# A two-layer mixer and expert kernel: the order of the opening, split output products, expert pages in halves

## The chip, the cores and the metric

The kernel runs on one core of a Trainium2 chip, all data in float32 but for a few bf16 masks. A core has five engines with a queue of their own: TensorE (PE in the profile; its weight loads stand apart as PEld), VectorE (DVE), ScalarE (ACT), GpSimd (POOL) and SyncE (SP), which issues most of the loads. Sixteen DMA engines move data between HBM, the large memory, and SBUF, the memory that the engines read. TensorE writes into PSUM. The metric is the device time of one execution in microseconds, the median of several runs.

## The reference

640 tokens (512 latent ones and 128 of a context) of 1024 channels go through two layers. Layer 0 mixes them by a convolution module and a differential attention side by side, layer 1 by a pooling mixer and a short gated convolution. Behind each mixer stands a mixture of 32 experts, two for each token:

```python
h = rmsnorm(x, p['g_norm1'][i]) * (1 + sc1) + sh1
if i % 2 == 0:
    m, k_cur, v_cur = even_mixer(h, p, j, i, rope, kv_in)   # cat([u, o]) @ w_out_e
else:
    m = odd_mixer(h, p, j)                                  # cat([yc, yd]) @ w_out_o
x = x + g1 * m
h = rmsnorm(x, p['g_norm2'][i]) * (1 + sc2) + sh2
y = hmoe(h.reshape(b * t, d), ...)      # top-1 group, top-2 expert
x = x + g2 * y.reshape(b, t, d)
...
hid = jax.nn.silu(xblk @ w_g[e]) * (xblk @ w_u[e])          # one expert, one block of tokens
return hid @ w_d[e]
```

Shifts, scales and gates come from `w_ada` products with a conditioning vector. An expert has three weight matrices of 2 MB (gate, up, down), 201 MB in a layer, and every one is read.

## The kernel before

The program is written engine by engine, each with its own instruction order and explicit semaphores; no scheduler moves anything. Tokens lie in five tiles of 128 (`NT`).

PSUM is used as four pairs of banks, A to D. A table written out by hand (`put`, from line 316) gives every use its pair and its place in that pair's order; `fill` and `take` wait by it. SBUF holds weights in nine slots of 2 MB. Each slot has a counter `slot_full`, raised by 16 for each load. SP's list `dense` names the pages of the dense weights in the order of their loads, and a page is loaded when the last product that read its slot is done (`page_free`).

**Opening.** ScalarE squares the five x tiles; VectorE first copies the turned parameters out of PSUM (line 1403), adds up the first modulation row (`rows_summed`, line 1083), then scales x (`normed`, line 1105). TensorE's opening stands from line 1826: products of `w_ada` pages (`ada_products`, line 1597), turns of the sums (`turned_sums`, line 1606), turns of normalized x, one of eight channel chunks after the other (`first_norm`, line 1620), then the projections (`project`, line 1656), which need the pages `in_e` 0 and 1 and the modulated chunks `hT` that ScalarE and VectorE write.

**Output products.** Behind attention VectorE normalizes the heads, TensorE turns them (`oT`, line 1940), ScalarE copies them out, and the router constant is made (line 1665). `tail` then multiplies tile after tile by the two halves of the output weights (`product`, line 1696: eight channel chunks of 512 columns, the first four from the convolution or pooling side, the last four from heads or the gated convolution). Behind each pair of products VectorE mixes the tile into x and normalizes it, ScalarE copies the turned tile, and TensorE makes its router logits (line 1689). In layer 1 TensorE waits for the last gated channels (`short_conv`) before `tail`.

**Routing.** VectorE makes ranks and tables in many small steps; TensorE adds small products (`ranks_and_table`, lines 1717 to 1732). `keep_busy` (line 1670) runs products into a place that no one reads.

**Experts.** A block is 64 tokens of one expert; four of the 32 positions have a second block, so a layer has 36. A block takes the gate and up products together (`gate_up`, line 1756: eight channel steps, gate and up beside each other), a turn of the hidden values (line 1763), the down products (line 1774). Three experts lie in SBUF. SP loads the next expert into a slot when TensorE is done with it:

```python
def expert(pos, st, done):
    e = sp.value_load(ORD[0:1, bass.ds(pos, 1)], min_val=0, max_val=NE - 1)
    sp.wait_ge(sig("gate_up_done", l), done)
    load(e, st, 0)
    load(e, st, 1)
    sp.wait_ge(sig("down_done", l), done)
    load(e, st, 2)
```

GpSimd gathers the blocks' tokens and scatters the results by indirect DMA.

## Time and profile before

| | us |
|---|---|
| median of three runs | 1820.04 (1819.36 to 1825.13) |
| the profiled execution, its own time | 1817.86 |
| its span, first to last instruction | 1815.6 |
| TensorE busy | 1559.9 (86%) |
| VectorE busy | 616.6 (34%) |
| ScalarE, GpSimd busy | 249.2 (14%), 247.2 (14%) |
| the SP queue's DMA packets, share of 16 engines' span | 67.6% |

The span falls into these stages: opening to 48 us, projections and convolution to some 200, attention to 365, output products and routing to 488, experts of layer 0 to 974, the mixer of layer 1 to 1184, output products and routing to 1296, experts to 1783, the end. The page cuts the span into 40 slices; in both expert stages its DMA row reads 9 (90% or more) in every slice and its rate row 419 to 421 GB/s in nearly all. A busy TensorE says little: matmuls are pipelined, and their time doubles when the granted clock falls from 1.00 (2.4 GHz) to 0.50 (1.2 GHz).

### The profile page before, as it was taken

To read this page: it belongs to the slowest core of one execution; us is meant where nothing else is said; L and a number is where in the kernel's file an instruction comes from. 1 tells how busy PE (TensorE), PEld (TensorE's weight loads), DVE (VectorE), ACT (ScalarE), POOL (GpSimd) and SP (SyncE) were. 2 spreads that over 40 slices of the span, in tenths; PEclk is the share of its full clock that TensorE was granted. 3 is DMA by queue.
4 is the path that set the end of the run, shared out by engine and by line. 5 is a ranking of instruction groups with operands and counts; after the bars stand their busy time and mean duration, and the time that the engine had idled before them with its cause. 6 is when DMAs were issued, how large, how long until landed. Compare 5 with 4: busy or idle time off the path is not lost.

```text
span 1815.6 us, 19429 instructions
## 1 busy us (share of the span) xinstructions
PE 1559.9 (86%) x6780; PEld 727.6 (40%) x6780; DVE 616.6 (34%) x1194; ACT 249.2 (14%) x497; POOL 247.2 (14%) x376
## 2 busy tenths in 40 slices
PE   4999896689898989898984799999898989898982
PEld 2445444545533333333332344545433333333330
DVE  2499546733622112122123220323521212211214
ACT  2111035521100000000002111011000000000001
POOL 0024020000121211211110001000112111121110
PEclk9999999989999999999997899999999999999996
DMA  9753423032599999999995653253699999999984
GB/s 343 270 186 140 156 77 151 24 151 81 190 420 419 419 420 420 420 420 420 421 408 225 216 191 135 93 232 131 258 420 420 419 419 418 419 420 420 419 364 191
DMA packets 115566, 534.12 MB, mean 294 GB/s; under 512 B 15581, under 2 KB 16406, under 8 KB 65066
## 3 DMA queue, kind: packets, MB, share of 16 engines
q1 hardware_dynamic: 92944, 493.45, 67.6%
q0 software_dynamic: 12032, 21.08, 3.1%
q10 hardware_dynamic: 10522, 18.64, 2.9%
q8 instruction: 48, 0.79, 0.2%
q14 instruction: 20, 0.16, 0.0%
HBM read 522.55 MB, written 27.33 MB: 303 GB/s over the span
## 4 chain that ended last, share of the span: by engine, by line
PE 53%; DMA 17%; DVE 4%; issue 3%; ACT 2%; SPq 1%; ACTq 0%; POOLq 0%; DVEq 0%
PE psum_pair_B L1756 22%; DMA scratch<-w_up 15%; PE psum_pair_C L1774 10%; PE psum_pair_C L1696 4%; PE psum_pair_B L1656 4%; PE psum_pair_D L1696 4%; PE psum_pair_A L1656 3%; PE psum_pair_D L1763 1%; DVE scratch L1341 1%; DMA weight_ring<-w_ada 1%; ACT scratch L874 1%; SPq L489 1%; PE psum_pair_C L1597 1%; PE psum_pair_C L1670 1%; PE psum_pair_D L1689 1%
## 5 line engine op out<-in xcount | busy, mean ns | idle before, releaser
L1756 PE MATMUL psum_pair_B<-weight_ring,gates_by_token 128*64 128x512 f32 x1408 | 322.9, 612 | 36.6 <-DMA weight_ring<-w_up 26.0
L1756 PEld LDWEIGHTS psum_pair_B<-weight_ring,gates_by_token 128*64 128x64 f32 x1408 | 119.0, 141 | 234.5 <-issue 234.5
L1341 DVE TENSOR_TENSOR scratch<-psum_pair_B,scratch 128x256 f32<-128x256 f32 x72 | 30.6, 425 | 534.7 <-ACT scratch L874 534.7
L1756 PE MATMUL psum_pair_B<-scratch,gates_by_token 128*64 128x512 f32 x896 | 199.6, 597 | 13.2 <-DMA scratch<-w_up 13.2
L1774 PE MATMUL psum_pair_C<-weight_ring,scratch 128*64 128x512 f32 x704 | 160.8, 597 | 24.9 <-issue 22.5
L682 POOL DMA_INDIRECT expert_rows<-scratch,scatter_rows x72 | 73.4, 1020 | 743.2 <-DVE scratch L1353 743.2
L1656 PE MATMUL psum_pair_A<-scratch,weight_ring 128*128 128x128 f32 (+1 forms) x512 | 143.5, 439 | 4.4 <-DVE scratch L1392 2.8
L874 ACT ACTIVATE scratch<-psum_pair_B 128x256 f32<-128x256 f32 x72 | 27.6, 383 | 866.2 <-PE psum_pair_B L1756 866.2
L1656 PE MATMUL psum_pair_B<-scratch,weight_ring 128*128 128x128 f32 (+1 forms) x512 | 142.2, 436 | 0.0
L1756 PEld LDWEIGHTS psum_pair_B<-scratch,gates_by_token 128*64 128x64 f32 x896 | 76.6, 138 | 132.2 <-issue 132.2
L1435 DVE SCALAR_TENSOR_TENSOR weight_ring<-weight_ring,params 128x655 f32<-128x655 f32 x120 | 117.2, 976 | 5.0 <-DVE gates_by_token L1083 0.9
L1774 PE MATMUL psum_pair_C<-scratch 128*64 128x512 f32 x448 | 102.3, 598 | 15.4 <-issue 11.3
L1353 DVE TENSOR_TENSOR scratch<-psum_pair_C,gates_by_token 128x512 f32<-128x512 f32 x72 | 49.8, 692 | 181.0 <-PE psum_pair_C L1774 181.0
L1656 PEld LDWEIGHTS psum_pair_A<-scratch,weight_ring 128*128 128x128 f32 x512 | 79.2, 192 | 71.2 <-issue 69.4
L1656 PEld LDWEIGHTS psum_pair_B<-scratch,weight_ring 128*128 128x128 f32 x512 | 78.5, 191 | 68.4 <-issue 68.4
L1774 PEld LDWEIGHTS psum_pair_C<-weight_ring,scratch 128*64 128x64 f32 x704 | 55.6, 136 | 99.8 <-issue 99.8
L671 POOL DMA_INDIRECT gates_by_token<-h_rows,gather_rows x68 | 71.1, 1045 | 60.0 <-POOL gather_rows L668 56.4
L1597 PE MATMUL psum_pair_C<-weight_ring,cond_T 128*32 128x512 f32 x368 | 49.5, 661 | 26.0 <-DMA weight_ring<-w_ada 20.4
L1744 PEld LDWEIGHTS psum_pair_A<-square_consts,gates_by_token 128*128 128x128 f32 x288 | 40.4, 209 | 57.7 <-issue 57.7
L1774 PEld LDWEIGHTS psum_pair_C<-scratch 128*64 128x64 f32 x448 | 33.7, 136 | 64.7 <-issue 59.0
L1083 DVE TENSOR_TENSOR gates_by_token<-psum_pair_C,gates_by_token 128x512 f32<-128x512 f32 x23 | 15.8, 686 | 124.1 <-PE psum_pair_C L1597 114.2
L1696 PE MATMUL psum_pair_C<-weight_ring 128*128 128x512 f32 x120 | 55.2, 611 | 0.0
(359 smaller groups left out, 1483.2 us busy)
## 6 DMA issues: line engine op xcount, KB each, us to landing
weight_ring<-w_gate SPq DMA_DIRECT2D x44, 2048.0 KB, 29.4
weight_ring<-w_up SPq DMA_DIRECT2D x44, 2048.0 KB, 33.7
weight_ring<-w_down SPq DMA_DIRECT2D x44, 2048.0 KB, 34.2
weight_ring<-w_ada SPq DMA_DIRECT2D x24, 2048.0 KB, 8.9
scratch<-w_up SPq DMA_DIRECT2D x20, 2048.0 KB, 28.3
scratch<-w_down SPq DMA_DIRECT2D x20, 2048.0 KB, 28.1
scratch<-w_gate SPq DMA_DIRECT2D x20, 2048.0 KB, 22.6
weight_ring<-w_in_e SPq DMA_DIRECT2D x5, 2048.0 KB, 13.2
```

The lines of the kernel that those rows point to most:

```text
L671: pool.indirect_dma_start(XG[par], None, h2_dram, bass.IndirectOffsetOnAxis(GI[par][:, :], 0), bounds_check=2 * TOK - 1, oob_is_err=False) ...
L682: pool.indirect_dma_start(y_dram, bass.IndirectOffsetOnAxis(SI[par][:, :], 0), YR[par], None, bounds_check=4 * TOK - 1, oob_is_err=False). ...
L874: act.activation(SIL[par], bank(B_, par, 256), ACT.Silu).then_inc(sig("silu", l), 1)
L1341: tt(HID[par], PB[B_][:, 512 * par + 256:512 * par + 512], SIL[par], ALU.mult).then_inc(sig("hidden", l), 1)
L1353: tt(YR[par], bank(C_, par), GS[par], ALU.mult).then_inc(sig("y_ready", l), 1)
L1435: stt(UO[:, j, :], UP[:, j, tap:tap + UOW], conv_wT[:, tap, j:j + 1], UO[:, j, :], ALU.mult, ALU.add).then_inc(sig("conv_step", j), 1)
L1597: ins = mm(p[rows, 0:512], condT[:, k, :], w[:, k, :], start=(k < 4), stop=(k >= 4))
L1656: ins = mm(p[:, cols], w[:, k, j * 128:(j + 1) * 128], hT[:, k, cols], start=(k == 0), stop=(k == DC - 1))
L1696: ins = mm(p[:, 0:512], cat(k)[:, t * 128:(t + 1) * 128], w[:, k, :], start=(k == 0), stop=(k == DC - 1))
L1744: ins = pe.transpose(PB[A_][:, 512 * par + c * 128:512 * par + (c + 1) * 128], XG[par][:, c:512:4], ident)
L1756: ins = mm(PB[B_][CAP * q:CAP * (q + 1), 512 * par:512 * par + 512].rearrange("p (u n) -> p u n", u=2), XGT[par][:, at:at + CAP], w[:, :, ...
L1774: ins = mm(PB[C_][CAP * q:CAP * (q + 1), 512 * par:512 * par + 512], HIDT[par][:, at:at + CAP], wd[:, j, 512 * q:512 * (q + 1)], start=(j ...
```

## The change

It has four parts. (1) In the opening VectorE scales x first and then copies the parameters; their three turns go to one PSUM pair with one signal; TensorE turns the chunks of x earlier among the `w_ada` products, and the fourth `w_ada` product moves from pair D to C. (2) `first_half` makes channel chunks 0 to 3 of the first tile's two output products ahead of the rest of them: in layer 0 one ahead of the head turns and one behind them, in layer 1 both ahead of the wait for `short_conv`. The router constant moves to pair A and, in layer 1, ahead of that wait; VectorE takes it after the first tile's mix. (3) Gate and up pages are loaded as two halves of 1 MB each; the first halves wait for the fourth channel step of the block that used the slot, the second ones for the eighth. The counters of those slots rise by 32 for each page. (4) Between ranks and table ten unread products run instead of eight.

```diff
@@ -293,7 +293,7 @@
-            fills = [f + (NE - s // 3 + 2) // 3 for s, f in enumerate(fills)]
+            fills = [f + (1 if s % 3 == 2 else 2) * ((NE - s // 3 + 2) // 3) for s, f in enumerate(fills)]
@@ -483,16 +481,23 @@
-                def load(e, st, kind):
+                def load(e, st, kind, halves=(0, 1)):
+
                     s = 3 * st + kind
-                    src = down_page(e) if kind == 2 else gate_page((wg, wu)[kind], e)
-                    sp.dma_start(gate_slot(s), src).then_inc(slot_full[s], 16)
+                    if kind == 2:
+                        sp.dma_start(gate_slot(s), down_page(e)).then_inc(slot_full[s], 16)
+                    else:
+                        for h in halves:
+                            sp.dma_start(gate_slot(s)[:, h, :], gate_page((wg, wu)[kind], e)[:, h, :]).then_inc(slot_full[s], 16)
...
+                    sp.wait_ge(sig("gate_up_half", l), done)
+                    load(e, st, 0, (0,))
+                    load(e, st, 1, (0,))
                     sp.wait_ge(sig("gate_up_done", l), done)
-                    load(e, st, 0)
-                    load(e, st, 1)
+                    load(e, st, 0, (1,))
+                    load(e, st, 1, (1,))
                     sp.wait_ge(sig("down_done", l), done)
                     load(e, st, 2)
@@ -1398,17 +1403,17 @@
-            for i, (dst, w) in enumerate(((P1, 32), (P2, 125), (P3, 12))):
-                p = take(dve, "par", i + 1)
-                took(dve.tensor_copy(dst[:, :], p[:, 0:w]), "par", i + 1)
-            for i in (1, 2, 3):
-                after(dve, "par", i)
+            normed(0)
+            p = take(dve, "par")
+            for at, dst, w in ((0, P1, 32), (512, P2, 125), (640, P3, 12)):
+                ins = dve.tensor_copy(dst[:, :], p[:, at:at + w])
+            took(ins, "par")
+            after(dve, "par")
...
             rows_summed(0, 0)
-            normed(0)
             rows_summed(0, 2)
@@ -1669,6 +1674,13 @@
+            def first_half(l, tag, cat, n):
+
+                w = page(pe, (tag, n))
+                p = fill(pe, "out", l, 0, n)
+                for k in range(4):
+                    mm(p[:, 0:512], cat(k)[:, 0:128], w[:, k, :], start=(k == 0), stop=False)
+
@@ -1692,7 +1704,7 @@
-                    for k in range(DC):
+                    for k in range(0 if t else 4, DC):
...
-                keep_busy(8)
+                keep_busy(10)
...
+                        if k == 3:
+                            ins.then_inc(sig("gate_up_half", l), 1)
                     ins.then_inc(sig("gate_up_done", l), 1)
...
-                            pe.wait_ge(slot_full[s0 + kind], nth + 16 * fulls[s0 + kind])
+                            pe.wait_ge(slot_full[s0 + kind], 2 * nth + 16 * fulls[s0 + kind])
@@ -1933,17 +1949,20 @@
+            cat0 = lambda k: catU[:, k, :] if k < 4 else oT[:, k - 4, :]
+            pe.wait_ge(sig("cat_u"), HC)
+            first_half(0, "out_e", cat0, 0)
             for h in range(HEADS):
...
-            pe.wait_ge(sig("cat_u"), HC)
+            first_half(0, "out_e", cat0, 1)
+            router_constant(0)
...
@@ -1993,9 +2012,11 @@
+            after(pe, "pool", HC - 1)
+            for n in range(2):
+                first_half(1, "out_o", lambda k: CAT[:, k, :], n)
+            router_constant(1)
             pe.wait_ge(sig("short_conv"), HC)
-            after(pe, "pool", HC - 1)
-            router_constant(1)
```

Line numbers of the changed program are a few higher. TensorE in the opening, before: L1597 are `w_ada` products, L1823 parameter turns, L1606 turns of sums, L1620 turns of x, L1656 the first projection.

```order
L1823 MATMUL psum_pair_A<-square_consts,scratch 128x12
L1606 MATMUL psum_pair_C<-square_consts,gates_by_token 128x2 x4
L1620 MATMUL psum_pair_A<-square_consts,weight_ring 128x128 x5
L1620 MATMUL psum_pair_B<-square_consts,weight_ring 128x128 x5
L1597 MATMUL psum_pair_C<-weight_ring,cond_T 32x512 x8
...
L1597 MATMUL psum_pair_D<-weight_ring,cond_T 32x512 x8
L1606 MATMUL psum_pair_C<-square_consts,gates_by_token 128x2 x8
L1620 MATMUL psum_pair_D<-square_consts,weight_ring 128x128 x5
L1620 MATMUL psum_pair_A<-square_consts,weight_ring 128x128 x5
L1620 MATMUL psum_pair_B<-square_consts,weight_ring 128x128 x5
L1656 MATMUL psum_pair_A<-scratch,weight_ring 128x512 x8
```

The same stretch of the changed program, where L1625 turns x, L1611 sums, L1602 are `w_ada` products and L1661 is the projection:

```order
L1837 MATMUL psum_pair_D<-square_consts,scratch 128x12
L1625 MATMUL psum_pair_A<-square_consts,weight_ring 128x128 x5
L1625 MATMUL psum_pair_B<-square_consts,weight_ring 128x128 x5
L1611 MATMUL psum_pair_C<-square_consts,gates_by_token 128x2 x4
L1625 MATMUL psum_pair_D<-square_consts,weight_ring 128x128 x5
L1602 MATMUL psum_pair_C<-weight_ring,cond_T 32x512 x8
...
L1625 MATMUL psum_pair_D<-square_consts,weight_ring 128x128 x5
L1625 MATMUL psum_pair_A<-square_consts,weight_ring 128x128 x5
L1602 MATMUL psum_pair_C<-weight_ring,cond_T 32x512 x8
L1611 MATMUL psum_pair_C<-square_consts,gates_by_token 128x2 x4
L1625 MATMUL psum_pair_B<-square_consts,weight_ring 128x128 x5
L1661 MATMUL psum_pair_A<-scratch,weight_ring 128x512 x8
```

Three chunks of x are turned ahead of the second `w_ada` product instead of two, and one instead of three is left behind the last one.

TensorE at the end of attention in layer 0, before: L1922 is the last attention product, L1940 turns the heads, L1665 is the router constant, L1696 the output products.

```order
L1922 MATMUL psum_pair_D<-scratch 128x128 x2
L1940 MATMUL psum_pair_A<-square_consts,scratch 128x128 x5
L1940 MATMUL psum_pair_B<-square_consts,scratch 128x128 x5
L1940 MATMUL psum_pair_A<-square_consts,scratch 128x128 x5
L1940 MATMUL psum_pair_B<-square_consts,scratch 128x128 x5
L1665 MATMUL psum_pair_D<-gates_by_token,square_consts 128x72
L1696 MATMUL psum_pair_C<-weight_ring 128x512 x4
L1696 MATMUL psum_pair_C<-weight_ring,scratch 128x512 x4
L1696 MATMUL psum_pair_D<-weight_ring 128x512 x4
L1696 MATMUL psum_pair_D<-weight_ring,scratch 128x512 x4
```

The same place in the changed program, where L1682 are the first halves and L1708 the rest:

```order
L1938 MATMUL psum_pair_D<-scratch 128x128 x2
L1682 MATMUL psum_pair_C<-weight_ring 128x512 x4
L1959 MATMUL psum_pair_A<-square_consts,scratch 128x128 x5
L1959 MATMUL psum_pair_B<-square_consts,scratch 128x128 x5
L1959 MATMUL psum_pair_A<-square_consts,scratch 128x128 x5
L1959 MATMUL psum_pair_B<-square_consts,scratch 128x128 x5
L1682 MATMUL psum_pair_D<-weight_ring 128x512 x4
L1670 MATMUL psum_pair_A<-gates_by_token,square_consts 128x72
L1708 MATMUL psum_pair_C<-weight_ring,scratch 128x512 x4
L1708 MATMUL psum_pair_D<-weight_ring,scratch 128x512 x4
```

The half on the convolution side of each product has moved ahead, one in front of the head turns and one behind them.

SP behind routing in layer 0, before: the first page of position 3 waits for all of the first block's gate and up products.

```order
L492 TENSOR_LOAD scratch [waits order_known]
L492 ISA x2
L489 ISA [waits gate_up_done_0]
L489 DMA weight_ring<-w_gate 128x2x2048
L489 DMA weight_ring<-w_up 128x2x2048
L489 DMA weight_ring<-w_down 128x2x2048 [waits down_done_0]
```

The same loads in the changed program:

```order
L494 TENSOR_LOAD scratch [waits order_known]
L494 ISA x2
L491 ISA [waits gate_up_half_0]
L491 DMA weight_ring<-w_gate 128x2048
L491 DMA weight_ring<-w_up 128x2048
L491 ISA [waits gate_up_done_0]
L491 DMA weight_ring<-w_gate 128x2048
L491 DMA weight_ring<-w_up 128x2048
L488 DMA weight_ring<-w_down 128x2x2048 [waits down_done_0]
```

Four loads of 1 MB stand where two of 2 MB stood, and two of them wait for the middle of the block.

## Rows read from the trace of the kernel before

**Rows 1.** Busy time by engine, granted clock, DMA share, GB/s of one stretch.

```profile
500.00:600.00 100.00, 91.76 (x426) 38.28 (x424) 22.51 (x48) 7.84 (x16) 19.74 (x32) 1.00 1.02 419
```

**Rows 2.** Timeline of TensorE: start, us, what [idle before]. First expert block, layer 0.

```profile
487.82 7.09 PE L1756 MATMUL psum_pair_B<-weight_ring,gates_by_token 128*64 128x512 f32 x32 [0.78 <-ACT gates_by_token L870]
```

**Rows 3.** Timeline of SP's queue: the first load into a used slot, both layers.

```profile
495.09 0.40 SPq L489 DMA_DIRECT2D weight_ring<-w_gate  x1
...
1303.73 0.39 SPq L489 DMA_DIRECT2D weight_ring<-w_gate  x1
```

**Rows 4.** Stretches as in rows 1, ahead of those loads' traffic, both layers.

```profile
492.80:496.00 3.20, 2.94 (x15) 1.23 (x12) 0.42 (x1) 0.76 (x2) 0.00 (x0) 1.00 0.02 3
...
1302.00:1304.60 2.60, 2.34 (x13) 1.05 (x10) 0.42 (x1) 0.74 (x2) 0.00 (x0) 1.00 0.00 0
```

**Rows 5.** Timeline of TensorE in the opening: first turn of x, first projection.

```profile
29.51 1.33 PE L1620 MATMUL psum_pair_A<-square_consts,weight_ring 128*128 128x128 f32 x5 [3.41 <-DVE weight_ring L1105]
...
48.21 8.89 PE L1656 MATMUL psum_pair_A<-scratch,weight_ring 128*128 128x512 f32 x32 [1.56 <-DVE scratch L1111]
```

**Rows 6.** Timeline of SP's queue: the second input page.

```profile
34.39 0.37 SPq L469 DMA_DIRECT2D weight_ring<-w_in_e  x1
```

**Rows 7.** DMA issues from 34.3 to 34.8: size, us from issue to landing.

```profile
weight_ring<-w_in_e SPq DMA_DIRECT2D x1, 2048.0 KB, 13.2
```

**Rows 8.** The page's groups: busy us, mean ns of one, idle before. The convolution.

```profile
L1435 DVE SCALAR_TENSOR_TENSOR weight_ring<-weight_ring,params 128x655 f32<-128x655 f32 x120 | 117.2, 976 | 5.0 <-DVE gates_by_token L1083 0.9
```

**Rows 9.** Timeline of TensorE: last block of layer 0.

```profile
957.65 8.79 PE L1756 MATMUL psum_pair_B<-weight_ring,gates_by_token 128*64 128x512 f32 x32 [2.67 <-issue]
```

**Rows 10.** Timeline of TensorE: end of attention, head turns, output products.

```profile
363.90 0.80 PE L1922 MATMUL psum_pair_D<-scratch 128*128 128x128 f32 x2 [0.45 <-DVE scratch L1495]
368.27 1.33 PE L1940 MATMUL psum_pair_A<-square_consts,scratch 128*128 128x128 f32 x5 [3.58 <-DVE scratch L1516]
...
374.77 5.13 PE L1696 MATMUL psum_pair_C<-weight_ring 128*128 128x512 f32 x8
...
390.04 3.60 PE L1696 MATMUL psum_pair_C<-weight_ring 128*128 128x512 f32 x8
393.47 3.60 PE L1696 MATMUL psum_pair_C<-weight_ring,scratch 128*128 128x512 f32 x8
```

**Rows 11.** Stretches as in rows 1: head turns, first products, table in routing.

```profile
368.30:373.00 4.70, 4.70 (x20) 3.88 (x20) 2.13 (x3) 2.38 (x3) 0.00 (x0) 0.50 1.02 427
374.30:377.70 3.40, 3.40 (x6) 1.85 (x7) 0.23 (x1) 0.00 (x0) 0.00 (x0) 0.50 1.00 414
...
476.80:483.50 6.70, 6.07 (x22) 4.99 (x23) 4.55 (x9) 0.00 (x0) 2.45 (x3) 0.50 0.00 0
```

**Rows 12.** Timeline of TensorE in routing: unread products (L1670), table, weights.

```profile
465.94 7.11 PE L1670 MATMUL psum_pair_C<-square_consts 128*128 128x512 f32 x16
475.14 1.29 PE L1726 MATMUL psum_pair_D<-scratch 128*128 128x56 f32 x10 [2.09 <-DVE scratch L1289]
477.43 2.38 PE L1726 MATMUL psum_pair_D<-scratch 128*128 128x56 f32 x10 [1.00 <-DVE scratch L1289]
479.61 2.04 PE L1670 MATMUL psum_pair_C<-square_consts 128*128 128x512 f32 x2
481.44 3.41 PE L1732 MATMUL psum_pair_D<-scratch 128*128 128x112 f32 x20
```

**Rows 13.** Timeline of VectorE behind the table: the row weights.

```profile
480.17 0.74 DVE L1299 TENSOR_TENSOR scratch<-scratch,small 128x560 f32<-128x560 f32 x1
```

**Rows 14.** Timeline of TensorE in layer 1: router constant, first router product.

```profile
1184.29 0.44 PE L1665 MATMUL psum_pair_D<-gates_by_token,square_consts 128*128 128x72 f32 x2 [1.72 <-DVE weight_ring L1569]
...
1212.97 1.87 PE L1689 MATMUL psum_pair_D<-router_weights,weight_ring 128*128 128x36 f32 x16
```

**Rows 15.** Timeline of VectorE in layer 1: the first tile's second normalization.

```profile
1208.50 1.23 DVE L1146 TENSOR_TENSOR gates_by_token<-x_residual,scratch 128x1024 f32<-128x1024 f32 x1 [8.46 <-DMA scratch<-modulation_rows]
```

**Rows 16.** Timeline of ScalarE in layer 1: the first turned tile.

```profile
1211.65 1.02 ACT L839 ACTIVATE weight_ring<-psum_pair_A 128x1024 f32<-128x1024 f32 x1 [10.09 <-DVE gates_by_token L1151]
```

39 lines of the change are left out of this document (19 added, 20 removed).

## Prediction

> **What bounds the kernel now.** I read the granted clock and the DMA rate in the page's forty slices first, then the expert stages, then backwards to what lets each stage begin, because the changed places are four stage beginnings.
>
> The two expert stages are more than half of the span, and the DMA engines bound them: between 500 and 600 us they are busy throughout at 419 GB/s [rows 1], while TensorE waits for pages. A stage of this kind ends as early as its stream of pages starts without a hole. It starts with one: the gate and up products of the first block begin at 487.82 and take 7.09 us [rows 2], the first page into a used slot is issued only when they are over, at 495.09 in layer 0 and 1303.73 in layer 1 [rows 3], and for 3.2 and 2.6 us before the pages flow again nothing moves (3 and 0 GB/s) [rows 4].
>
> At the opening, TensorE waits 3.41 us for the normalized x, and begins the first projection at 48.21 when VectorE has written the last channel chunk [rows 5]. The second input page, which the same instruction also needs, was issued at 34.39 and took 13.2 us: it landed at 47.59 [rows 6, 7]. So only 0.6 us of that start are VectorE's. Behind it 120 convolution steps of 976 ns stand on VectorE [rows 8]: whatever the projections gain or lose is passed on to all that follows.
>
> A burst of products that starts after a gap is dearer: the 32 records of a gate and up product took 7.09 us at 487.82 [rows 2] and 8.79 us at 957.65, after 2.67 us without work [rows 9]. That is 1.7 us for one cold start, and I use it as the price below.
>
> At the end of attention TensorE ends its last product at 364.70, waits 3.58 us, turns the heads, and starts the first tile's output products at 374.77; the second tile's start at 390.04 [rows 10]. The granted clock is 0.50 (1.2 GHz) during the turns and the first products [rows 11]. In routing, TensorE runs eight unread products, idles 2.09 us, and does the rest of the table at 0.50 [rows 11, 12], while VectorE makes the row weights behind the table [rows 13]. In layer 1 it idles 1.72 us before the output products [rows 14], but VectorE cannot go on with the first tile before 1208.50, when modulation rows have landed [rows 15], so ScalarE's turned tile comes at 1211.65 to 1212.67 [rows 16].
>
> **Opening.** VectorE normalizes x ahead of the parameter copies, and TensorE turns the first chunks ahead of the sums that wait for VectorE. The page decides: its place in the queue and the bytes ahead of it are the same, so the start can move from 48.21 to about 47.7, a gain of 0.5. But TensorE has then done its turns earlier: by the new order its last products before the page are one group of sums and five turns, spread over some 5 us. That is emptier than the gap ahead of 957.65, so I expect the projection to begin at 1.2 GHz and lose 1.7. Net **+1.2 us**; bounds -0.5 (no fall of the clock) and +2.4 (a fall that lasts longer than in [rows 9]). The merged parameter transposes and copies are the same six instructions; their PSUM pair is free.
>
> **Output products of layer 0.** Half of two products (16 of 32 records) now stands before the head turns and half between them and the rest. From 364.70 to 390.04 are 25.3 us. At full clock a half product is 3.43 (from 390.04 to the next half in the same pair, 393.47 [rows 10]), so the two products are 13.7; I take 2.8 for the four turns (half of the 4.7 that they take at half clock [rows 11], and 0.4 for the ScalarE copies between them) and 0.3 for the router constant: 16.8. The engine has no wait left in it: the weight pages landed long before, and the normalized heads are there when the first half product is over. One cold start costs 1.7, ending at 383.2, a gain of 6.8. If the clock stays at 1.2 GHz through the half product and two turns, 4.6 are lost instead and the gain is 4.0. I take **-5.5**, between them, since the half product is dense work. VectorE takes the router constant after the first tile's mix instead of before it: its 0.23 us have no one waiting; the modulation rows are issued when the heads are copied, about as early as now.
>
> The Trainium skill ("TensorE: Matmul & The Clock Gate", PE-mode transpose) says that transposes do not count as TensorE work as matmuls do for raising the clock. The trace agrees: 4.70 of 4.70 us busy with turns at 0.50 [rows 11], and the rise came only behind the products. By it the gain is nearer 6.8, by a count of all work nearer 4.0.
>
> **Output products of layer 1.** The first halves of both products need only the pooled channels and fill the 1.72 us. TensorE then reaches the first router product about 1.7 us earlier, where it needs the turned tile that ScalarE has at 1212.67; it started at 1212.97 [rows 14, 16]. Those rows arrive with the expert pages of the same moment, which the change does not thin out. So **-0.2**, bounds 0 and -1.7.
>
> **Ten unread products.** Eight take 7.11 us, 0.89 each [rows 12]; two more end 0.3 us before the table's first inputs, so they delay nothing. If the idle 2.09 shrinks to 0.3, the clock should not fall. The second table group then takes 1.29 instead of 2.38, the unread product behind it 0.9 instead of 1.8, and the weight products some 2.25 instead of 3.2 [rows 12], 3.0 in all. Not all of it arrives: the row weights are there 1.1 us behind the table (480.91 against 479.81) [rows 12, 13], of which the unread product fills 0.9, and the gathered rows follow the table too. I take 0.5 off, and 0.7 in layer 1: **-2.5 in layer 0 and -2.3 in layer 1**. Bounds 0 (it falls all the same) and -3.0.
>
> **Pages in halves.** SP now waits for the fourth of eight channel steps, loads the first halves of gate and up, then waits for the eighth. The first issue comes half of 7.09, 3.5 us, earlier. Two halves are 2.1 MB, 5.0 us at 419 GB/s, and cover the 3.5 us until the second halves. The hole in [rows 4] goes: 3.2 us and the ramp behind it in layer 0, 2.6 and its ramp in layer 1. Since the DMA engines bound all that follows, the stages end **3.5 and 3.2** earlier. What is late next is the stream itself. SP's added wait has only that expert's own loads behind it. The semaphore increments in mid-product ride on matmuls, as at every product's end today, and cost nothing. Bounds: 0 and -3.9 a layer.
>
> **Sum.** +1.2 - 5.5 - 0.2 - 4.8 - 6.7 = -16.0. The profiled execution took 1817.86 (its span 1815.6 and 2.3 around it), which gives 1801.9; the median of the three runs shown is 2.2 higher, so the predicted time is 1820.0 - 16.0 = **1804.0**.
>
> **Rivals.** *The clock falls in routing all the same.* The table products are small, and TensorE still pauses 1.00 us between their groups. Then 4.8 are missing: 1808.8. Against it: the pause left is half of what preceded today's fall. *The hole closes but comes back*: the added issues eat the 6.7 gained, 1810.7, because each load keeps a wait of its own. Against it: the rate of 419 is held while SP's issues take 0.4 each. *Slower*: the halved pages move at a lower rate, each further load leaving the DMA engines empty for a moment. There are two more for each of 29 experts in two saturated layers, 116; at 0.14 us each they eat the whole 16.0 (a rate of 408 instead of 419 on the 243 MB of halved pages), and at the 0.40 us that SP takes for an issue [rows 3] they cost 46, giving 1850. Against it: loads wait in the queue long before they move, and today's three loads an expert leave no gap in the rate. *No gain at the front*: the cold opening takes 2.4 and the attention end gives 4.0, which with the rest as forecast is 1806.7; it lies in the range.
>
> The Trainium skill ("DMA: Bandwidth & Descriptors", Measured) gives 341 GB/s for a transfer of 1 MB and says to batch to at least that. By 341 instead of 419 for the halved two thirds of the bytes the stages would be an estimated 130 us longer. That table is of transfers issued from GpSimd; no row here shows such a drop, and today's pages of 2 MB already move at 419.
>
> **How the numbers follow.** Forecast with all parts (1804): 0.56. Clock falls in one or both routings (1806 to 1809): 0.22. No gain from the halves (1810.7): 0.09. That with the clock falling too (1815.5): 0.05. Slower by empty moments (1820 to 1850): 0.05. Other, better than forecast (opening without the cold start, both 6.8 and 3.9): 0.03. The low end is 1820.0 - 20.0 = 1800, from values at or near the better bounds (-0.5, -6.8, -0.2, -5.5, -7.0); the high end 1812 takes in the case without the halves' gain. This measurement can tell 0.3% (5.5 us) from no change: faster than that needs a time under 1814.5, and holds in the first three cases and the last; with something off for what I have not seen, 0.85; within 0.3%, 0.09; slower, 0.06.
>
> **What would show it.** Right: in the changed profile no hole of DMA traffic after the first expert block and a first issue 3.5 us after the block's start; the first projection at about 47.7 with a granted clock of 0.5; the second tile's output products about 25.3 - 5.5 = 20 us after the last attention product; the granted clock at 1.00 through the table products. Wrong: a DMA rate under 419 in the stages; a hole that has only moved; routing still at 0.5; or output products of layer 0 that wait for the heads.

## The result: 1808.0 us, and the profile after

The changed kernel takes 1808.0 us in the median of seven runs (1798.2 to 1815.1), beside 1819.36 of the kernel before; the ratio is 0.9931 (95% interval 0.9911 to 0.995); the medians lie 11.4 us apart. The time lies in the range 1800 to 1812, 4 us above the 1804.0 that was forecast. The profiled execution took 1804.19 (its span 1802.0), 13.6 under the span of before.

The span can be cut at starts that both timelines of TensorE show. Each row is the time between two of them; the last column is the term of the prediction.

| stretch | before | after | change | predicted |
|---|---|---|---|---|
| start to first modulation product | 19.14 | 20.20 | +1.1 | none |
| from there to the second projection | 39.75 | 42.53 | +2.8 | +1.2 |
| to the last attention product's end | 305.81 | 305.79 | 0.0 | 0 |
| to the second tile's output products | 25.34 | 18.25 | -7.1 | -5.5 |
| to the first table product | 85.10 | 85.08 | 0.0 | 0 |
| to the first expert block | 12.68 | 10.29 | -2.4 | -2.5 |
| to the last expert block, layer 0 | 469.83 | 466.34 | -3.5 | -3.5 |
| to the end of layer 1's projections | 224.93 | 224.38 | -0.5 | 0 |
| to the first table product, layer 1 | 100.87 | 102.16 | +1.3 | -0.2 |
| to the first expert block | 13.00 | 10.79 | -2.2 | -2.3 |
| to the last expert block, layer 1 | 470.33 | 467.43 | -2.9 | -3.2 |
| to the end | 48.83 | 48.73 | -0.1 | 0 |

Four of the seven terms came within 0.3 us. The rows behind them follow. In them a burst of products is called cold where it starts at the granted clock of 0.50 (1.2 GHz), and warm at 1.00 (2.4 GHz). Timeline of TensorE, opening of the changed kernel (start, us, what, [idle before and what ended it]); it answers to [rows 5]:

```profile
36.32 1.42 PE L1611 MATMUL psum_pair_C<-square_consts,gates_by_token 128*128 128x2 f32 x8 [1.44 <-DVE gates_by_token L1088]
...
39.90 3.64 PE L1602 MATMUL psum_pair_C<-weight_ring,cond_T 128*32 128x512 f32 x16
...
47.33 1.30 PE L1625 MATMUL psum_pair_B<-square_consts,weight_ring 128*128 128x128 f32 x5 [1.86 <-ACT scratch L784]
50.29 10.66 PE L1661 MATMUL psum_pair_A<-scratch,weight_ring 128*128 128x512 f32 x32 [1.65 <-DVE scratch L1116]
```

The fourth modulation product in the kernel before, in the same view:

```profile
39.89 1.92 PE L1597 MATMUL psum_pair_D<-weight_ring,cond_T 128*32 128x512 f32 x16
```

Behind the wait of 1.44 us the clock is at half speed: the modulation product at 39.90 takes 3.64 us instead of 1.92, the sums that it feeds are late, and the projection waits for VectorE's last chunk, not for the page. It then starts cold once more: 10.66 in place of 8.89.

The same view at the end of attention, against [rows 10]:

```profile
367.72 0.80 PE L1938 MATMUL psum_pair_D<-scratch 128*128 128x128 f32 x2 [0.45 <-DVE scratch L1500]
368.31 5.09 PE L1682 MATMUL psum_pair_C<-weight_ring 128*128 128x512 f32 x8
373.23 0.71 PE L1959 MATMUL psum_pair_A<-square_consts,scratch 128*128 128x128 f32 x5
...
376.24 3.60 PE L1682 MATMUL psum_pair_D<-weight_ring 128*128 128x512 f32 x8
...
386.77 3.60 PE L1708 MATMUL psum_pair_C<-weight_ring 128*128 128x512 f32 x8
```

The first half product takes the place of the 3.58 us wait and pays the one cold start (5.09 instead of 3.60); the turns behind it take 0.71 where they took 1.33.

Routing of layer 0, against [rows 12]:

```profile
462.66 8.83 PE L1675 MATMUL psum_pair_C<-square_consts 128*128 128x512 f32 x20
471.85 1.29 PE L1738 MATMUL psum_pair_D<-scratch 128*128 128x56 f32 x10 [0.37 <-DVE scratch L1294]
474.15 1.32 PE L1738 MATMUL psum_pair_D<-scratch 128*128 128x56 f32 x10 [1.00 <-DVE scratch L1294]
...
482.14 7.09 PE L1768 MATMUL psum_pair_B<-weight_ring,gates_by_token 128*64 128x512 f32 x32 [0.78 <-ACT gates_by_token L875]
```

The idle time ahead of the table is 0.37, and the second group takes 1.32 where it took 2.38. Next the timeline of SP's queue, against [rows 3], and the stretches behind it (busy time of the engines, granted clock, DMA share, GB/s), against [rows 1, 4]:

```profile
485.99 0.36 SPq L491 DMA_DIRECT2D weight_ring<-w_gate  x1
```

```profile
485.60:489.00 3.40, 3.40 (x18) 1.20 (x14) 0.00 (x0) 0.00 (x0) 0.00 (x0) 1.00 0.74 264
489.00:492.00 3.00, 2.14 (x12) 1.27 (x12) 1.65 (x5) 0.98 (x2) 0.00 (x0) 1.00 1.00 423
...
500.00:600.00 100.00, 93.41 (x434) 39.06 (x432) 22.84 (x48) 7.85 (x16) 19.52 (x31) 1.00 1.01 419
```

The first load is issued 3.85 us after the block's start, where it took 7.27 before; the hole of 3 GB/s is a dip to 264 (246 in layer 1), and the stage runs at 419 as before. Last, TensorE and VectorE in layer 1's output products, against [rows 14, 15]:

```profile
1194.40 7.03 PE L1708 MATMUL psum_pair_D<-weight_ring 128*128 128x512 f32 x16
1202.77 2.40 PE L1701 MATMUL psum_pair_D<-router_weights,weight_ring 128*128 128x36 f32 x16 [1.33 <-ACT weight_ring L844]
1204.97 8.40 PE L1708 MATMUL psum_pair_C<-weight_ring 128*128 128x512 f32 x16
```

```profile
1198.54 1.23 DVE L1151 TENSOR_TENSOR gates_by_token<-x_residual,scratch 128x1024 f32<-128x1024 f32 x1 [9.93 <-DMA scratch<-modulation_rows]
```

The idle 1.72 us ahead of these products are gone and have come back as 1.33 ahead of the first router product. There they cost the clock: the router product takes 2.40 us in place of 1.87 [rows 14], and the products behind it 8.40 in place of 7.03.

### The profile page after: what moved, and what is told of

Same layout as the page of the kernel before. It is cut to its first block, busy times and chain, and to the rows that moved or that the text cites. A ratio compares the mean times of both kernels' runs of the same rounds, so it can differ in the third digit from the quotient of the medians.

```text
span 1802.0 us, 19786 instructions
## 1 busy us (share of the span) xinstructions
PE 1558.7 (87%) x6788; PEld 723.3 (40%) x6788; DVE 616.6 (34%) x1194; ACT 249.1 (14%) x497; POOL 247.6 (14%) x376
## 4 chain that ended last, share of the span: by engine, by line
PE 49%; DMA 15%; SPq 7%; DVE 4%; issue 3%; ACT 2%; ACTq 0%; POOLq 0%; DVEq 0%
PE psum_pair_B L1768 20%; DMA scratch<-w_up 10%; PE psum_pair_C L1788 10%; SPq L491 6%; PE psum_pair_B L1661 4%; PE psum_pair_A L1661 3%; PE psum_pair_C L1708 3%; PE psum_pair_D L1708 3%; DMA weight_ring<-w_gate 2%; PE psum_pair_D L1777 1%; DMA scratch<-modulation_rows 1%; DVE scratch L1346 1%; DMA weight_ring<-w_ada 1%; SPq L488 1%; ACT scratch L879 1%
## 5 line engine op out<-in xcount | busy, mean ns | idle before, releaser
L1661 PE MATMUL psum_pair_A<-scratch,weight_ring 128*128 128x128 f32 (+1 forms) x512 | 145.2, 442 | 4.5 <-DVE scratch L1397 2.8
L1661 PE MATMUL psum_pair_B<-scratch,weight_ring 128*128 128x128 f32 (+1 forms) x512 | 142.2, 436 | 0.0
L1358 DVE TENSOR_TENSOR scratch<-psum_pair_C,gates_by_token 128x512 f32<-128x512 f32 x72 | 49.8, 692 | 181.0 <-PE psum_pair_C L1788 181.0
L1661 PEld LDWEIGHTS psum_pair_A<-scratch,weight_ring 128*128 128x128 f32 x512 | 79.8, 194 | 72.5 <-issue 70.5
L1661 PEld LDWEIGHTS psum_pair_B<-scratch,weight_ring 128*128 128x128 f32 x512 | 78.4, 191 | 68.5 <-issue 68.5
L1602 PE MATMUL psum_pair_C<-weight_ring,cond_T 128*32 128x512 f32 x384 | 52.3, 668 | 27.3 <-DMA weight_ring<-w_ada 21.8
L1353 DVE SCALAR_TENSOR_TENSOR gates_by_token<-gates_by_token,small 128x512 f32<-128x512 f32 x72 | 54.1, 751 | 2.6
```

The costliest lines, as they stand in the source:

```text
L1353: stt(GS[par], G2[:, 1], SWC[par][:, 1:2], GS[par], ALU.mult, ALU.add).then_inc(sig("slot_gate", l), 1)
L1358: tt(YR[par], bank(C_, par), GS[par], ALU.mult).then_inc(sig("y_ready", l), 1)
L1602: ins = mm(p[rows, 0:512], condT[:, k, :], w[:, k, :], start=(k < 4), stop=(k >= 4))
L1661: ins = mm(p[:, cols], w[:, k, j * 128:(j + 1) * 128], hT[:, k, cols], start=(k == 0), stop=(k == DC - 1))
```

## Experiments

The times of executions spread: the changed kernel's from 1798 to 1815. The stretches of the table are the sharper measure, and each run below gave them for one execution. A time is the median of its runs; the kernel before took 1819.2 to 1819.7 beside them.

### One part undone

**Whole pages.**

```diff
...
-                    sp.wait_ge(sig("gate_up_half", l), done)
-                    load(e, st, 0, (0,))
-                    load(e, st, 1, (0,))
                     sp.wait_ge(sig("gate_up_done", l), done)
-                    load(e, st, 0, (1,))
-                    load(e, st, 1, (1,))
+                    load(e, st, 0)
+                    load(e, st, 1)
...
```

> The changed kernel with gate and up pages loaded whole again, all else kept. My theory, that the halves only close the hole in DMA traffic behind the first expert block: the hole is back in both layers, the stretch from the first expert block's start to the last one's grows from 466.3 to about 469.8 us in layer 0 and from 467.4 to about 470.3 in layer 1, and the time rises by 6.4 us, from 1808 to about 1814. Rival, that the added loads eat part of what the closed hole gives: both stretches grow by less than 2 us, and the DMA rate inside the stages is above the 419 GB/s that both kernels show.

Measured: 469.46 and 469.95 us, 3.1 and 2.5 more than with halves, 5.6 together; 1810.5 us (1807 to 1820). The hole is back, here ahead of the first whole page's traffic (stretch as above):

```profile
496.00:499.20 3.20, 2.98 (x16) 1.21 (x12) 0.42 (x1) 0.56 (x2) 0.00 (x0) 1.00 0.01 5
```

My theory holds by the stretches: the ten executions with halves of 1 MB on record take 465.9 to 467.1 us in layer 0 and 466.5 to 469.0 in layer 1, all less than these. The rival falls by them too, and the rate from 500 to 600 us is 418 here. The median rose by only 2.5, which is within the spread. This run's profiled execution was its longest, 1819.61, and shows a part of what the spread is made of. The clock over two stretches of attention that no part of the change touches, this kernel first and the changed kernel behind it:

```profile
200.00:250.00 50.00, 43.72 (x184) 22.86 (x182) 12.41 (x22) 7.80 (x14) 5.64 (x4) 0.86 0.47 169
250.00:300.00 50.00, 42.21 (x115) 19.70 (x113) 25.90 (x39) 14.91 (x26) 7.61 (x6) 0.91 0.26 105
```

```profile
200.00:250.00 50.00, 42.95 (x181) 21.63 (x182) 15.84 (x23) 8.13 (x15) 8.16 (x6) 0.97 0.47 168
250.00:300.00 50.00, 41.18 (x142) 21.18 (x142) 26.49 (x51) 19.03 (x37) 5.07 (x4) 0.97 0.34 137
```

From the second projection to attention's end it took 313.1 us where the changed kernel took 305.8, with the same program there.

**Eight unread products.**

```diff
-                keep_busy(10)
+                keep_busy(8)
```

> The changed kernel with eight unread products ahead of the table in place of ten. My theory, that only the two added products keep the clock up: TensorE idles about 2.1 us ahead of the table, the granted clock falls to 0.50 behind it in both layers, the stretch from the first table product to the first expert block goes from 10.3 to about 12.7 us in layer 0 and from 10.8 to about 13.0 in layer 1, and the time rises by 4.6 us. Rival, that the clock fell in the kernel before because of where the rest of the program had put this stretch in time: it stays at 1.00 in one layer or both, and those stretches stay under 11 us.

Measured: 12.66 and 12.47 us; the clock fell in both layers, as in the kernel before. My theory holds for the stretches (+2.4 and +1.7). The time did not show it: 1808.16, where 4.6 more were expected. So what two products are worth rests on the stretches alone.

**Layer 1's first halves late.**

```diff
+            pe.wait_ge(sig("short_conv"), HC)
             after(pe, "pool", HC - 1)
             for n in range(2):
                 first_half(1, "out_o", lambda k: CAT[:, k, :], n)
             router_constant(1)
-            pe.wait_ge(sig("short_conv"), HC)
```

> The changed kernel with the first halves of layer 1's output products, and the router constant, behind the wait for the last gated channel again. In the changed kernel the stretch from the end of the last projection to the first table product of layer 1 is 102.15 us, in the kernel before 100.9. My theory, that the work done early only moved TensorE's gap to the first router product, where 1.33 us without work cost the clock (the products behind it took 8.40 in place of 7.03): the stretch is back at 100.9 or less, and the time falls by about 1.3 us. Rival, that the lower clock there has another cause: the stretch grows by the 1.7 us of the wait, to 103.8.

Measured: 100.88 us, and 1806.71. The part of the change for layer 1 costs 1.3 us where it stands. It does so in more than one execution: five other runs that keep it and neither fill the wait nor touch the rows or the size of the packets (whole pages, eight products, the old opening, the opening kept busy, the table) wait 1.40 to 1.80 us at the first router product, and their stretches are 102.25 to 104.33. The run also showed what was not expected: with ten products, the clock fell in layer 1's table, and the stretch behind it was 13.02 us. Timeline of TensorE:

```profile
1270.08 1.29 PE L1738 MATMUL psum_pair_D<-scratch 128*128 128x56 f32 x10 [0.37 <-DVE scratch L1294]
1272.38 2.21 PE L1738 MATMUL psum_pair_D<-scratch 128*128 128x56 f32 x10 [1.00 <-DVE scratch L1294]
```

The waits are those of the execution in which it did not fall (0.36 and 1.00).

**The old opening.** `normed(0)` behind the first row sum again, parameters in three pairs, TensorE's order as before.

```diff
...
             rows_summed(0, 0)
+            normed(0)
             rows_summed(0, 2)
...
             ada_products(0, 0)
             feature_parameters()
-            first_norm(0, (0, 1))
             turned_sums(0, 0)
-            first_norm(0, (2,))
+            first_norm(0, (0, 1))
...
```

> The changed kernel with the opening of the kernel before (order of TensorE and VectorE, pairs of PSUM). In the changed kernel 42.53 us lie between the first product of a modulation page and the second projection, in the kernel before 39.75. My theory, that the new order leaves TensorE with two thin places that cost it the clock: the stretch is back at 39.75, and the time falls by 2.8 us. Rival, that the loss is a matter of the single execution (its first product was 1.06 us later too): the stretch stays between 41 and 43, or lies far from 39.75 on either side, and the time moves by under 1 us.

Measured: 41.40 us, which lies in the rival's range, and 1803.84, which does not: it is 4.2 less. The first projection is warm (10.67 us to the second), but this execution lost its clock in the turns ahead of it and started it at 49.80. Over all runs the old opening gives 39.75 and 41.40, the new one in nine executions 41.65 to 44.62, with a mean of 43.1: by two executions against nine, the new order costs about 2.5 us. That the empty places are what costs is shown by the fillers below, not by this run.

### Waits filled, and the cause behind one of them

**Opening kept busy.**

```diff
+            keep_busy(2)
             turned_sums(0, 1)
             first_norm(0, (5, 6))
             ada_products(0, 3)
+            keep_busy(1)
             turned_sums(0, 3)
+            keep_busy(2)
             first_norm(0, (7,))
+            keep_busy(2)
```

> The changed kernel with seven unread products in the places of its opening where TensorE waits (two ahead of the third turned sum, one ahead of the fourth, two ahead of the last turned chunk, two ahead of the first projection). Five executions with the new opening so far show a granted clock of 0.50 for 10 to 14 us of the stretch from 32 to 56 us, and 12.4 to 13.7 us from the first to the second projection, where the old opening takes 10.67. My theory, that the loss is TensorE's empty places: the clock stays at 1.00 from 33 us on, the first projection takes 8.9 in place of 10.7 and begins by 48.5, the first projection's stretch is 10.7, and the stretch from first modulation product to second projection falls from 42.5 to about 39. Rival, that the sums and chunks are late of themselves: the first projection begins at 50 as before, and only the 1.8 us of the cold first projection are won.

Measured: 40.66 us, 1804.16. The products that I put last stood behind a wait for VectorE, and so in the way:

```profile
47.79 1.95 PE L1675 MATMUL psum_pair_C<-square_consts 128*128 128x512 f32 x4 [1.38 <-DVE scratch L1116]
49.59 8.81 PE L1661 MATMUL psum_pair_A<-scratch,weight_ring 128*128 128x512 f32 x32
```

The first projection is warm, 8.81, but it starts at 49.59 and not by 48.5, and the 1.9 us won are what the rival said. The rows show why: VectorE's chunk was there at 47.79, and my two last products ran in front of the projection. Whether the sums are late of themselves this run leaves open; a version below, without products in that place, settles it.

**Layer 1's first router product.**

```diff
                     product(t, 1)
+                    if l and t == 1:
+                        keep_busy(2)
                     if t:
                         router_product(t - 1)
```

> The changed kernel with two unread products ahead of the first router product of layer 1, where TensorE waits 1.33 us for ScalarE's turned tile. My theory, that this wait is the early halves' 1.7 us come back and costs the clock behind it: the clock stays at 1.00 from 1200 to 1210, the products behind the router product take 7.1 in place of 8.4, and the stretch from the first router product to the table goes from 72.26 back to about 70.5 us; together with the 0.45 us by which two products overfill the wait the time falls by about 1.3 us. Rival, that the early halves are what costs, by another way (the order in PSUM): the stretch stays at 72.

Measured: 30.15 and 70.58 us, 1.4 less than in the changed kernel; 1801.78. The clock is 1.00 there, and the products behind take 7.12:

```profile
1201.11 1.98 PE L1701 MATMUL psum_pair_D<-router_weights,weight_ring 128*128 128x36 f32 x16
1202.91 7.12 PE L1708 MATMUL psum_pair_C<-weight_ring 128*128 128x512 f32 x16
```

**Between the table's groups.**

```diff
                 for i in range(10):
+                    if i == 5:
+                        keep_busy(1)
                     pe.wait_ge(sig("one_hots"), 2 * l + i // 5 + 1)
```

> The changed kernel with one more unread product between the two groups of table products, where TensorE waits 1.00 us for VectorE. With ten unread products ahead of the table the clock stayed at 1.00 there in seven of eight executions seen (four kernels, two layers) and fell in layer 1 of one. My theory, that the wait between the groups is the thin place left: with it filled the clock is 1.00 in both layers, the stretches from the first table product to the first expert block are 10.3 and 10.8 us as in the changed kernel, and the time is within 1 us of 1808. Rival, that the product is in the way: the stretches grow by up to 0.9 us.

Measured: 10.28 and 10.75 us; the time, 1803.43, is 4.6 under the changed kernel's and not within 1. The product is not in the way. One execution is no proof of the rest; the three kernels here that have this product kept the clock in both layers. The nine executions with ten products and none in between kept it in layer 0 nine times, in layer 1 five times, so that three in layer 1 do not show that this wait was the thin place, the one that costs the clock. With eight products (the kernel before, and the run with eight) it fell in both layers of both.

**Modulation rows ahead of the pages.**

```diff
                     load(0, 0, 2)
+                    sp.wait_ge(sig("rows_back", 3), 64)
                     page_free(sp, owners[0])
                     load(0, 0, 0)
```

> The changed kernel in which SP, in layer 1, waits for the last modulation rows before it loads the three expert pages that were issued beside them (6 MB, pages of experts 1 and 3, not needed for 100 us). In the changed kernel the rows' six transfers of 0.5 MB, issued from 1172.96 on, take until 1198 beside those pages, VectorE waits 9.9 us for them, TensorE waits 1.33 us ahead of the first router product, and the clock falls. My theory, that the rows share the DMA engines with the pages and nothing else holds them: they land within some 10 us, VectorE's wait goes, TensorE has no wait there, from the end of the last projection to the first router product are 28.6 us in place of 29.9 and from there to the table 70.5 in place of 72.3, together 3 us, and the experts of layer 1 begin and run as before. Rival, that the rows are slow of themselves (a row is sent to 128 partitions): they land after 1190 all the same, and nothing is won.

Measured: 28.42 and 70.46 us, 3.3 less than in the changed kernel; 1795.25 (ratio 0.9875, 0.9854 to 0.9896). VectorE's wait for the rows is gone, and with it TensorE's. The DMA issues of that stretch (size, us to landing) of the changed kernel and of this one, then VectorE and TensorE of this one:

```profile
scratch<-modulation_rows ACTq DMA_DIRECT2D x4, 512.0 KB, 18.3
```

```profile
scratch<-modulation_rows ACTq DMA_DIRECT2D x4, 512.0 KB, 9.5
```

```profile
1184.26 1.23 DVE L1152 TENSOR_TENSOR gates_by_token<-x_residual,scratch 128x1024 f32<-128x1024 f32 x1 [0.24 <-DVE scratch L1146]
```

```profile
1196.69 1.87 PE L1702 MATMUL psum_pair_D<-router_weights,weight_ring 128*128 128x36 f32 x16
```

The rival falls: the rows were slow because 6 MB of pages moved beside them. The median fell by more than these 3.3 us; a further 4.5 in this execution lie at layer 1's start (219.9 in place of 224.4), as in two kernels without this edit (220.1 and 220.7). Without the edit SP issues its next load only at the end of that stretch (1172.89 in the changed kernel), so the added wait behind it cannot have made the difference.

### More loads

**Quarters by partitions.**

```diff
...
-                            sp.dma_start(gate_slot(s)[:, h, :], gate_page((wg, wu)[kind], e)[:, h, :]).then_inc(slot_full[s], 16)
+                            for part in (slice(0, 64), slice(64, 128)):
+                                sp.dma_start(gate_slot(s)[part, h, :], gate_page((wg, wu)[kind], e)[part, h, :]).then_inc(slot_full[s], 16)
...
```

> The changed kernel with each half page of gate and up loaded by two loads of 0.5 MB (partitions 0 to 63 and 64 to 127), so that an expert takes eight such loads and the down page in place of four and the down page. My theory, that loads wait in the queue long before they move and cost the stream nothing: the DMA rate from 500 to 600 us stays at 419 GB/s and the stretches from the first to the last expert block stay within 1 us of 466.3 and 467.4 us. Rival, the fifth case of my prediction, that each further load leaves the DMA engines empty for a moment: 4 further loads for each of 29 experts, 116 a layer, at 0.14 us each make the stretches 16 us longer, and the rate is near 405.

Measured: 847 and 859 us, 2571 us in all (2524 to 2594). Neither theory had this. The DMA engines are busy throughout and move 258 GB/s:

```profile
500.00:600.00 100.00, 65.39 (x272) 25.18 (x270) 14.28 (x30) 4.91 (x10) 12.34 (x20) 0.83 1.02 258
```

116 loads at 0.14 us would explain 16 of the 380 us, so I cut the same bytes another way.

**Quarters by columns.** As above, with `part` of 1024 columns of all 128 partitions.

> The changed kernel with each half page of gate and up loaded by two loads of 0.5 MB again, but cut by columns: all 128 partitions, 4 KB from each in place of 8. The cut by partitions 0 to 63 and 64 to 127 gave 258 GB/s from 500 to 600 us in place of 419 and stretches of 847 and 859 us in place of 466. My theory, that what was dear there was the half set of partitions and not the number of loads: the rate is 400 GB/s or more and the stretches at most 490 us. Rival, the fifth case of my prediction (each further load leaves a gap): the rate is far under 400 and the stretches again over 600 us.

Measured: 477.2 and 477.7 us, 1821.72 in one run.

```profile
500.00:600.00 100.00, 91.05 (x414) 37.74 (x412) 22.15 (x47) 7.86 (x16) 17.67 (x30) 0.98 1.02 412
```

The half set of partitions was the cost, not the number of loads. The 116 further loads a layer cost 10.9 and 10.3 us, 0.09 each at most, and part of that may belong to the packets of 4 KB; that was not separated.

This run shows one thing more, for the run on modulation rows. It has no added wait in SP's order, and the same 6 MB of pages move beside the rows, but in packets of 4 KB. The rows land 13.6 us after their issue (median of the last four, 18.3 in the changed kernel), TensorE has no wait at layer 1's first router product, and the two stretches are 28.41 and 70.47 us, as with the rows first:

```profile
1211.15 1.87 PE L1702 MATMUL psum_pair_D<-router_weights,weight_ring 128*128 128x36 f32 x16
```

### Versions that beat both

**Ten places filled.** The expectation calls them eight; its list and the edit have ten. The changed kernel with five places of the opening filled, one product ahead of layer 1's first router product, and

```diff
+                if j == 1:
+                    keep_busy(5)
                 ada_products(1, j)
...
+                    if i == 5:
+                        keep_busy(1)
                     pe.wait_ge(sig("one_hots"), 2 * l + i // 5 + 1)
...
+                    if last:
+                        for _ in range(4):
+                            mm(PB[D_][:, 256:512], ident, SQ[:, 0:256], start=True, stop=True)
                     if nth is not None:
...
+                if i == 1:
+                    for _ in range(4):
+                        mm(PB[D_][:, 512:1024], ident, SQ[:, 0:512], start=True, stop=True)
                 if i < NU:
                     scores(i)
```

> The changed kernel with unread products in eight places where TensorE waits and where executions so far showed the clock fall behind the wait: five in the opening (one ahead of the second, third and fourth turned sum, two ahead of the last turned chunk, one behind it), the first router product of layer 1 (one), between the two groups of table products (one), ahead of the second modulation product in the keys' projections (five, a wait of 5.4 us), ahead of the second scores of attention (four, a wait of 4.2 us), and ahead of the last expert block of each layer (four of half width, a wait of 2.4 us). My theory, that the clock behind a wait is what these places cost, and that a filler shorter than the wait is free: first projection at 48, 10.7 us to the second, second projection to the end of attention about 304 in place of 305.8 to 313, both tables at 1.00 (10.3 and 10.8 us), last blocks 7.1 in place of 8.6; together 6 to 9 us under the changed kernel's 1808, near 1800. Rival, that most of these places are covered by other engines: under 3 us are gained, and the last blocks' gain is lost behind the scatter.

Measured: 1797.12 us (1795.4 to 1800.3), ratio 0.9886 (0.9863 to 0.9909). The opening takes 38.32 us, second projection to attention's end 304.1, both tables hold, and the last block is warm. By the medians 10.9 us are gained, by the profiled executions 5.8, and the rival's limit of 3 falls. Layer 1's expert stage took 469.0 us here against 467.4, which I cannot explain.

```profile
47.15 8.89 PE L1662 MATMUL psum_pair_A<-scratch,weight_ring 128*128 128x512 f32 x32 [1.58 <-DMA weight_ring<-w_in_e]
...
940.84 7.09 PE L1773 MATMUL psum_pair_B<-weight_ring,gates_by_token 128*64 128x512 f32 x32 [0.45 <-issue]
```

With no clock lost, the page releases the first projection, as the prediction had it, and the sums are not late of themselves. One filler failed: with everything earlier, the rows of layer 1 came later still against it, TensorE waited 1.90 us behind the one product, and the clock fell (31.33 and 72.29 us).

**Fillers, and rows first.** The version before with the filler of layer 1 replaced by the wait of the rows' run, two more products in attention and seven in layer 1's start.

```diff
+                if i in (1, 2):
+                    for _ in range((4, 2)[i - 1]):
+                        mm(PB[D_][:, 512:1024], ident, SQ[:, 0:512], start=True, stop=True)
...
+                    if i == 1:
+                        keep_busy(7)
                     if i < 8:
                         ada_products(1, 4 + i)
```

> The unread products of the version before it, which took 1797, but none at layer 1's first router product; there the modulation rows go ahead of the pages instead, as in the run beside it; two more unread products ahead of the third scores of attention, and seven ahead of the second modulation product of layer 1, where TensorE waits 8 us for a page. My theory: 3 us from layer 1's output products and 2 to 3 us from layer 1's start, about 1792. Rival, that layer 1's start is bound by VectorE and ScalarE there and the rows by themselves: 1796 to 1798.

Measured: 1789.06 us (1786.6 to 1789.1), ratio 0.9836 (0.9819 to 0.9853). It beats both kernels, and it spreads least: the mean granted clock of its five executions is 0.975 to 0.977, of the changed kernel's seven 0.921 to 0.965. Against the version before it, layer 1's start takes 219.4 us in place of 224.8 and its output products 98.9 in place of 103.6. Three kernels without the seven products took 219.9 to 220.7 at layer 1's start, so what these products are worth is not shown.

## Why the prediction came out as it did

**Pages in halves: right.** -3.5 and -2.9 against -3.5 and -3.2, and whole pages bring 3.1 and 2.5 of it back; over ten executions with halves the stretches average 466.3 and 467.1, 3.5 and 3.3 under the kernel before. The rate stayed 419, so the case "slower by empty moments" falls here. Twice the loads, with smaller packets, cost at most 0.09 us a load, under the 0.14 at which it would have decided; the change's own 58 further loads a layer cost far less, since at 0.09 they would have eaten 5 us, more than the whole gain. The Trainium skill's figure for 1 MB ("DMA: Bandwidth & Descriptors", Measured: 341 GB/s) does not show in a queue that is always full: 419 with loads of 1 MB.

**Ten unread products: right in size, half right in layer 1.** -2.4 and -2.2 against -2.5 and -2.3 in the profiled execution; that this execution kept the clock in layer 1 is luck, since of nine only five did. The rival "the clock falls all the same" was priced well and placed too rarely: layer 1 fell in four of nine executions, layer 0 in none. The step that failed is "if the idle 2.09 shrinks to 0.3, the clock should not fall": 0.36 with the 1.00 between the groups still made it fall at times.

**Output products of layer 0: the mechanism right, the size at its better end.** The step that took -5.5 allowed for a clock that stays low through the half product and two turns. It rose inside the half product, and the turns ran at full speed: -7.1, 0.3 past the bound of -6.8. That the half product raised it and the turns didn't have to is all the rows show; whether turns alone would have is not settled, and that "a count of all work" leads to 4.0 does not follow from the working. No run undoes this part; the thirteen executions that have it take 17.6 to 18.3 us there, where the kernel before took 25.3.

**Opening: the sign right, the size too small, +2.8 against +1.2, beyond the bound of 2.4.** Two steps failed. The cold start of the first projection was priced at 1.7 from [rows 9]; it cost 1.8 here and up to 3.0 in other executions (13.67 us to the second projection against 10.67). And "the page decides" holds only where the clock was not lost earlier: here a half-speed modulation product delayed the sums, and the projection waited for VectorE until 50.29. I looked for thin places only ahead of the page, not at 35 us, where the earlier order makes TensorE wait for VectorE's sums. Of the nine executions with this opening, five start the projection at 49.8 to 52.3 us, and four at 47.6 to 48.2, and these four pay 2.7 to 3.0 for the cold start. The run with the rows first comes nearest to the forecast's own case: its fourth modulation product runs at full speed (1.92), the page is the last to come, and the stretch is still 1.9 longer than before (41.65):

```profile
47.86 11.57 PE L1662 MATMUL psum_pair_A<-scratch,weight_ring 128*128 128x512 f32 x32 [2.74 <-DMA weight_ring<-w_in_e]
```

**Layer 1: wrong, +1.3 against -0.2.** The step named the rows as what is late, and bounded the cost by 0 and -1.7: a gap that moves was taken to be free. But the products in front of the wait no longer covered it. Moving TensorE ahead of a transfer that does not move made the wait 1.33 us: 0.5 us were won up to the router product (29.90 in place of 30.39), and the clock behind it cost 1.8 (72.25 in place of 70.47). Undoing it, filling it, and taking the rows out of the pages' way each gave it back. With the rows in time the early halves do gain: 98.88 us in place of 100.87, somewhat more than the bound of 1.7.

**The sum.** -16.0 was forecast. In the profiled execution +1.6 (opening), +1.5 (layer 1) and -1.6 (layer 0's output) were missed, +0.5 in the other terms, and +0.4 in places that the change doesn't touch: -13.6. The median is 4 us above the forecast: 2.3 are these misses, 2.3 more come from the profiled execution, which lies 3.8 under the changed kernel's median where that of before lies 1.5 under its own, and 0.7 go off, since the median of the kernel before is 1819.4 in seven runs and was 1820.0 in the three that the forecast started from. That the misses of 1.6 and 1.5 on one side met 1.6 on the other is luck.

## What to carry to other kernels

Work moved ahead of a wait gains only if the wait ends earlier too: look where the saved time stands next, and whether TensorE then starts cold behind it. A wait that cannot be removed is worth filling with unread products a little shorter than it, placed in front of the wait and not behind it; where a transfer ends it, see first what moves beside that transfer. Read a change of under 1% from stretches between the same two starts, not from one time.

## What the runs showed of the hardware that was not expected

- Loads onto partitions 0 to 63 and 64 to 127 ran at 258 GB/s, where loads over all 128 of the same size ran at 412. The Trainium skill says so ("SBUF — State Buffer", Door 1: The DMA port swizzle): a half set reaches half of the ports. The Trainium skill says too ("SBUF — State Buffer", "Can I just issue two DMAs to hit both halves?") that two such loads serialize. By the 218 GB/s that Door 1 of the Trainium skill gives, for the two thirds of the bytes that were cut, and its 436 for the rest, an estimate is 262 GB/s; the run's 258 agrees.
- Behind the same waits (0.36 and 1.00 us, between short products) TensorE was granted 1.2 GHz in some executions and not in others: in layer 1's table in four of nine, with 13.0 us instead of 10.8 behind them. Behind 1.33 to 1.80 us at layer 1's first router product it fell in all six executions that left the wait as it is.
- Six transfers of modulation rows (3 MB) took twice as long beside 6 MB of pages issued at the same moment, 18.3 against 9.5 us in the median of the last four. Between 1178 and 1190 us of the changed kernel the pages' queue and the rows' queue moved 472 and 469 packets, but 3.34 and 1.71 MB. With the pages cut by columns, between 1187 and 1195, it was 407 and 400 packets, and 1.50 and 1.47 MB. So the two queues shared the DMA engines by packets, and the size of the packets set the shares of bytes.
